# Four middle head pairs of a layer: an engine loop replaced by straight code

## What is computed

```python
x = layer_norm(ALPHA * x + 0.5 * swiglu(x, ffn1_w_in, ffn1_w_out), ln1_g, ln1_b)
z = x @ w_in
u, zr = z[..., :D_POOL], z[..., D_POOL:]
pool_out, pool_new = pool_mixer(u, pool_hist, pos0, pool_w, pool_scale)
rwkv_out, shift_new, wkv_new = rwkv7_mixer(zr, shift_prev, wkv_prev, ...)
x = layer_norm(ALPHA * x + concat(pool_out, rwkv_out) @ w_out, ln2_g, ln2_b)
h = ALPHA * x + 0.5 * swiglu(x, ffn2_w_in, ffn2_w_out)
h = h + sigmoid(h @ ple_gate_w + ple_gate_b) * (p @ ple_w)
x = layer_norm(h, ln3_g, ln3_b)
```

```python
def wkv_step(S, inp):
    r_t, w_t, k_t, v_t, a_t, b_t = inp
    sa = jnp.einsum('bhvk,bhk->bhv', S, a_t)
    S = S * w_t[:, :, None, :] + sa[..., None] * b_t[:, :, None, :] + v_t[..., None] * k_t[:, :, None, :]
    y = jnp.einsum('bhvk,bhk->bhv', S, r_t)
    return S, y
```

## Time and profile before

| | |
|---|---|
| median of three runs | 3031.05 us (3028.4 to 3035.96) |
| time of the profiled execution | 3029.19 us |
| span of the profiled execution, first to last instruction | 3027.2 us |
| TensorE busy with matmuls | 2735.7 us, 90% of the span |
| TensorE weight loads | 2623.4 us, 87% |
| GpSimd, VectorE, ScalarE busy | 1445.2, 1092.2 and 696.9 us |
| granted TensorE clock, mean | 0.955 of full speed |

### The profile page before, as it was taken

The page is one execution under the profiler, slowest core; times in us unless marked ns, Lnnn a source line. Parts: engine busy times, 40 slices in busy tenths (PEclk is TensorE's granted clock), DMA queues, the critical chain, the costliest instruction groups (busy, mean ns, idle before and its releaser), DMA issues.

```text
span 3027.2 us, 68787 instructions
## 1 busy us (share of the span) xinstructions
PE 2735.7 (90%) x27640; PEld 2623.4 (87%) x27640; DVE 1092.2 (36%) x1448; ACT 696.9 (23%) x1193; POOL 1445.2 (48%) x932
## 2 busy tenths in 40 slices
PE   8999989888887899999799999898888888999995
PEld 8999979776776799999699999797777777999994
DVE  3222047545553422211432210575545434222124
ACT  3221021233421322200232210212343203221013
POOL 5555645422213455555555555454222145555553
PEclk9999999889997999999999999898999989999997
DMA  4232322100001132332222322120000012223321
GB/s 147 88 90 82 89 60 85 36 3 4 3 19 43 56 90 83 97 86 77 85 73 87 90 85 85 60 84 22 4 3 4 17 57 63 90 85 93 90 73 57
DMA packets 64112, 192.66 MB, mean 64 GB/s; under 512 B 11712, under 2 KB 14016, under 8 KB 63936
## 3 DMA queue, kind: packets, MB, share of 16 engines
q1 hardware_dynamic: 59904, 185.95, 20.5%
q10 hardware_dynamic: 4032, 4.08, 0.4%
HBM read 186.88 MB, written 3.12 MB: 63 GB/s over the span
## 4 chain that ended last, share of the span: by engine, by line
PE 73%; issue 14%; POOL 6%; DVE 4%; ACT 3%; DVEq 0%; ACTq 0%; DMA 0%; POOLq 0%; SPq 0%
PE ps L519 64%; PE ps L575 4%; PE ps L534 2%; POOL w_lo L464 1%; DVE xl L1192 1%; PE ps L679 1%; POOL w_hi L462 1%; DVE y L1188 1%; DVE rs L1177 0%; POOL nt L391 0%; POOL tA L397 0%; POOL Lb L423 0%; POOL nt L389 0%; PE ps L694 0%; ACT xh L887 0%
## 5 line engine op out<-in xcount | busy, mean ns | idle before, releaser
L519 PE MATMUL ps<-xh,w_hi 128*128 128x272 f32 x4032 | 848.7, 292 | 104.3 <-POOL w_lo L464 49.0
L464 POOL TENSOR_TENSOR w_lo<-w_raw,w_hi 128x1024 fp32r<-128x1024 f32 (+3 forms) x380 | 854.8, 2249 | 31.7
L519 PE MATMUL ps<-xh,w_lo 128*128 128x272 f32 x4032 | 838.7, 290 | 0.0
L519 PE MATMUL ps<-xl,w_hi 128*128 128x272 f32 x4032 | 838.4, 290 | 0.0
L462 POOL TENSOR_SCALAR w_hi<-w_raw 128x1024 fp32r<-128x1024 f32 (+3 forms) x380 | 374.0, 984 | 865.7 <-PE ps L519 856.4
L519 PEld LDWEIGHTS ps<-xh,w_hi 128*128 128x128 f32 x4032 | 639.2, 190 | 118.4 <-DVE xl L1192 54.9
L519 PEld LDWEIGHTS ps<-xl,w_hi 128*128 128x128 f32 x4032 | 640.8, 191 | 0.0
L519 PEld LDWEIGHTS ps<-xh,w_lo 128*128 128x128 f32 x4032 | 636.3, 190 | 0.0
L1144 DVE TENSOR_TENSOR hf<-sg,ps 128x544 f32<-128x544 f32 x88 | 63.5, 722 | 708.3 <-PE ps L519 708.3
L519 PE MATMUL ps<-hh,w_hi 128*128 128x272 f32 x1472 | 305.5, 289 | 0.0
L519 PE MATMUL ps<-hl,w_hi 128*128 128x272 f32 x1472 | 303.6, 287 | 0.0
(11 more groups left out here) (242 smaller groups left out, 3202.8 us busy)
## 6 DMA issues: line engine op xcount, KB each, us to landing
w_raw<-in_w1i SPq DMA_DIRECT2D x88, 512.0 KB, 3.5
w_raw<-in_w2i SPq DMA_DIRECT2D x88, 512.0 KB, 3.5
w_raw<-in_wz SPq DMA_DIRECT2D x44, 512.0 KB, 3.5
w_raw<-in_w1o SPq DMA_DIRECT2D x32, 448.0 KB, 3.4
w_raw<-in_w2o SPq DMA_DIRECT2D x32, 448.0 KB, 3.3
w_raw<-in_w1o SPq DMA_DIRECT2D x16, 512.0 KB, 3.5
w_raw<-in_wo SPq DMA_DIRECT2D x16, 512.0 KB, 3.6
w_raw<-in_w2o SPq DMA_DIRECT2D x16, 512.0 KB, 3.5
```

The costliest lines, as they stand in the source:

```text
L464: pool.tensor_tensor(w_lo[k][:, 0:nk, :], w_raw[k][:, 0:nk, :], w_hi[k][:, 0:nk, :].bitcast(F32), ALU.subtract).then_inc(w_split, 1)
L519: mm = pe.matmul(ps[:, 2 * pair + h, 0:HT], w[:, j, :], x[:, k0 + j, h * HT:(h + 1) * HT], start=(part == 0 and j == 0 and q == 0), stop=( ...
```

## The change

In `heads` the engine loop over pairs 1 to 4 becomes a Python loop over the same pairs, so that each engine's program holds the body four times, one after the other, with the pair as a constant. The order of the instructions and all the semaphores that they wait for stay the same. The loop over the two layers stays an engine loop.

```diff
             half_a(l, 0, True, False, True)
             half_b(l, 0, True, False)
-            with eng.Fori(0, NPAIR - 2) as q:
-                half_a(l, q + 1, True, True, True)
-                half_b(l, q + 1, True, True)
+            for q in range(1, NPAIR - 1):
+                half_a(l, q, True, True, True)
+                half_b(l, q, True, True)
             half_a(l, NPAIR - 1, True, True, False)
             half_b(l, NPAIR - 1, False, True)
             half_a(l, NPAIR, False, True, False)
```

## The result

| | before | after |
|---|---|---|
| median | 3030.44 us (4 runs) | 3000.51 us (4 runs, 2994.59 to 3005.33) |
| ratio | | 0.9897, 95% interval 0.9875 to 0.992 |
| time of the profiled execution | 3029.19 us | 3005.33 us |
| its span | 3027.2 us | 3003.5 us |

The change made the kernel faster by 29.9 us between the medians, 1.0%, and by 23.9 us between the two profiled executions. The kernel before has one execution more here than in the table ahead of the prediction. Timed once more in six executions beside the kernel before, the ratio was 0.9908 (0.9889 to 0.9927).

The account below looks back on a forecast made before the run. TensorE was taken to bound the kernel, with pauses at jumps back in the heads. Six jumps gone, -19.1, plus clock falls, +2.4, gave -16.7 us: 3014.4 us forecast, range 3009 to 3023 us.

Parts of the forecast that it names:

- What bounds the heads, and the jump: TensorE delays the heads' end one for one; removing six jumps back in the pair loop gains 19.09 us.
- E64: TensorE's first step of a pair, 20 weight loads: 3.65 us gap behind a jump back, 1.12 us forecast without one.
- No new stops: Straight code in the heads adds no fetch stops, 0 us; the rival, new stops ending slower, had 0.05.
- the prediction's own signs of being wrong: A border still over 3 us, an "issue" gap inside a pair, or heads 17 us shorter with longer dense phases.
- The clock: TensorE's clock may still fall behind 1.5 of six new straight borders, +2.4 us; rival of nearly all falling, 0.12.
- Register arithmetic with the pair: Constant pair saves instructions before waits and addresses: taken as 0, at most 0.3 us in eight iterations, 2.4 us.
- The row it rested on: One step in the pair has the same 1.37 us gap with the pair in a register and without.

Follow-up runs that it names:

- TensorE alone straight: Against the kernel before, only TensorE's program has the four middle pairs as straight code with constants, the other engines keep the loop: 3008.72 us, ratio 0.9925.
- the short loops in front: Changed kernel plus, on TensorE before E64 of pairs 2, 3 and 4, a three-trip loop around one wait long met: 3001.12 us, ratio 0.9918.
- the kernel with the added wait: Changed kernel plus a TensorE wait for VectorE's copy of lora_st before E64 of pairs 2, 3 and 4, without a jump: 3009.28 us, ratio 0.9944.
- the second profile: Profile from running the changed kernel again, unaltered, beside the kernel before: 3002.26 us over 6 runs, ratio 0.9908.
- The run with two trips: Changed kernel with the middle pairs in a two-trip engine loop over two pairs each, pair in a register, one jump per layer: 3010.55 us, ratio 0.9936.
- the runs with single engines: Kernel before with only some engines straight: TensorE 3008.72 us; all but TensorE 3020.49 and 3019.01; TensorE with ScalarE 3008.15; TensorE with VectorE 3003.30.
- the one with layers written out: Changed kernel with the loop over the two layers also written out on all five engines: 2997.77 us, ratio 0.9906.

## Why the prediction was right or wrong

*What bounds the heads, and the jump.* Right. The pauses sat on TensorE's path; all six went to 1.12 us. TensorE alone straight gained 20.9 us, which holds its share of the arithmetic too; a jump that goes back a few instructions costs nothing, one that goes back over two pairs (4.38 and 4.64 us before E64) costs more than one over one.

*No new stops.* Wrong in one place. Queue 14 brought 14 packets more, not 24, and they cost nothing that shows. But one of the prediction's own signs of being wrong came: a gap ended by "issue" inside a pair, 0.83 us in pass 3 of both layers, worth 0.6 us each. Pair 5 of the kernel before, from which the 0 us was taken, has no such gap. The place moves with the code: with the short loops in front it stands one group of matmuls earlier (0.51 us, line 622, layer 0), and the kernel with the added wait has none. Why it is there stays open.

*The clock.* The size came out by luck. The prediction had 1.5 falls of 1.6 us, 2.4 us. The changed passes are 2.5 us longer in sum than eight passes like the first of their layer. Of that only about 1.5 us is the clock, one fall of six, in pass 4 of layer 0; some 1.2 us is the stop, and small differences between passes take the rest back. In the second profile no border had a fall.

*Register arithmetic with the pair: this step failed.* The prediction took 0 and set the bound at 0.3 us a pass. Measured: 52.15 to 51.16 and 52.38 to 51.42, 0.98 us a pass, 7.8 us in eight. The run with two trips shows that it is the register and not the jump: with the register and no jump the same passes are 0.6 to 1.0 us longer than with constants, and by the runs with single engines it lies on TensorE (0.35 to 0.57), VectorE (0.4) and ScalarE (0.0 to 0.2). The row it rested on was true and still is: the 1.37 us before that step are the same before and after, and its stretch from 848.21 to E64, 10.77 us, is 10.46 after. The error was to take a bound from 10 us of the pass for the 52 of it. The places that lengthened it lie elsewhere in the pass. The kernel before could not show them against straight code, since pair 5 has other flags in `half_a` and `half_b`; a bound over the whole pass was not to be had from one piece, and the range should have allowed 0.3 us for each 10.

The sum by the measured terms: jumps -19.1, arithmetic -7.8, fall and stops left +2.5, pair 5 -1.9 (1.67 of it in layer 0, where pair 5 had a fall before and none after) are -26.2 us for the heads, unrounded; the other stretches of the profiled execution gave back 2.5 to make 23.7. The median of the first set lies 6 us lower still.

*That remainder goes with the clock of whole executions; why that differs stays open.* The stretches around the passes (first pair of a layer, tail, norm) come in lengths that differ by 3 to 7 us between profiles of kernels with the same order of work there: from the first norm of layer 1 to its first landmark 217.5 to 224.5 us, from pair 5's landmark to the norm 92.9 to 97.2. The first of these goes with its granted clock: 217.6 to 218.3 us in the five profiles with 0.91 there, 224.5 in the changed kernel's first, the lowest with 0.88. Executions of one kernel spread over 4 to 18 us in the same way: of the first four of the changed kernel, 2995.93 and 2994.59 us have a mean clock of 0.960, 3005.33 and 3005.10 have 0.958 and 0.956. The profiled one is the slowest of them, so this pair of profiles shows less than the medians; only the passes are read to 0.1 us. I can't say whether these stretches' clock depends on the code: the kernel with two trips gained 8.4 us in its passes and 19 in its median, the one with layers written out 17.5 and 30.

## What to carry to other kernels

Look for a step at the top of a long engine loop whose idle time the profile ends with "issue", and compare it with the same step at the loop's entry and exit, best over the whole iteration: the difference, times the jumps, is what the jumps cost. A loop over one wait had no such difference here. Where small operations of several engines hand over to each other, count the address and count arithmetic in front of each one too; it was 1 us of 52 here, and could be read only over the whole pass. A bound from a piece of a pass is a bound for that piece. And read the granted clock of each pass before a difference is put down to it: here two passes that looked like a fall of the clock were a stop.

## What was not expected of the hardware

A fully constant program was not the fastest in its chain: 51.9 to 52.3 us a pass against 51.2 with the layer in a register, and TensorE ran more register instructions in it, not fewer. The pause of a jump grew from 3.1 to 3.7 us to 4.4 and 4.6 when the loop body doubled. The clock fell to 0.50 for some 3 us behind idle stretches of only 2.70 us, in four cases of six. And straight code had a stop of its own, 0.83 us in the middle of a group of equal matmuls, at the same place in both layers.
